# Half of one gate tile, a reordered square, moved sums and inner values, and two unread products in a decoder in fp32

## The reference, cut to what matters

```
x = x + 0.5 * swiglu_ffn(rmsnorm(x, ffn1_norm), w_gu, w_down)      # four FFNs in all, 2816 wide
x = x + mixer(rmsnorm(x, mix_norm))
# rglru, in the first mixer; w_r, w_i are 8 blocks of 64 x 64 each
r  = sigmoid(x @ w_r + b_r);  ig = sigmoid(x @ w_i + b_i)
a  = exp(-8 * r * softplus(-lam))
u  = sqrt(1 - a * a) * (ig * x);  h = scan(a, u)
# mlstm: h = (p @ v) / max(|sum p|, exp(-m)), p = exp(d - m) * (q @ k.T)
# second: mod = silu(c) @ ada_w + ada_b;  h = modulate(rmsnorm(ctx or x), mod) ...
```

## Time and profile before

| | us |
|---|---|
| median of 3 runs | 2051.26 (2048.83 to 2052.66) |
| the profiled execution | 2049.97 |
| its span, first to last instruction | 2048.2 |
| PE busy | 2018.8 |
| POOL busy | 1686.9 |
| DVE, ACT busy | 1156.3, 1147.0 |
| granted TensorE clock | 0.999 of full |

### The profile page before, as it was taken

The page is one execution under the profiler, slowest core; times in us unless marked ns, Lnnn a source line. Parts: engine busy times, 40 slices in busy tenths (PEclk is TensorE's granted clock), DMA queues, the critical chain, the costliest instruction groups (busy, mean ns, idle before and its releaser), DMA issues. The chain is left out here.

```text
span 2048.2 us, 38776 instructions
## 1 busy us (share of the span) xinstructions
PE 2018.8 (99%) x15616; PEld 1905.6 (93%) x15616; DVE 1156.3 (56%) x1985; ACT 1147.0 (56%) x1951; POOL 1686.9 (82%) x787
## 2 busy tenths in 40 slices
PE   9999999999999999999999999999999999999998
PEld 9999889999999977999889999999999998888886
DVE  7777635776577554444656315998788522222224
ACT  6445765435444466444754545457887655555555
POOL 4998778999899756889766586798777799999997
PEclk9999999999999999999999999999999999999999
DMA  9565446666766432666453355355454456555554
GB/s 356 211 223 185 151 169 229 232 210 231 270 249 223 183 127 102 252 218 222 167 196 128 144 184 217 105 186 186 165 166 165 166 186 201 194 192 194 195 193 146
DMA packets 80755, 395.28 MB, mean 193 GB/s; under 512 B 11100, under 2 KB 12252, under 8 KB 52448
## 3 DMA queue, kind: packets, MB, share of 16 engines
q1 hardware_dynamic: 80608, 393.28, 54.6%
HBM read 392.19 MB, written 1.05 MB: 192 GB/s over the span
## 5 line engine op out<-in xcount | busy, mean ns | idle before, releaser
L475 POOL TENSOR_TENSOR ring_low<-ring_raw,ring_high 128x2048 fp32r<-128x2048 f32 x204 | 998.5, 4913 | 230.3 <-ACT ring_high L461 230.2
L2668 POOL TENSOR_TENSOR peerS_low<-peerS_raw,peerS_high 128x512 fp32r<-128x512 f32 x510 | 655.6, 1310 | 88.0 <-ACT peerS_high L2819 87.7
L522 PE MATMUL bank<-keep_xThigh,ring_high 128*128 128x256 f32 x2080 | 581.6, 280 | 4.3 <-POOL ring_low L475 3.1
L523 PE MATMUL bank<-keep_xTlow,ring_high 128*128 128x256 f32 x2080 | 576.2, 277 | 0.0
L524 PE MATMUL bank<-keep_xThigh,ring_low 128*128 128x256 f32 x2080 | 576.2, 277 | 0.0
L461 ACT ACTIVATE ring_high<-ring_raw 128x2048 fp32r<-128x2048 f32 x204 | 391.1, 1917 | 271.9 <-PE bank L524 251.2
L522 PEld LDWEIGHTS bank<-keep_xThigh,ring_high 128*128 128x128 f32 x2080 | 391.0, 188 | 8.0 <-issue 5.1
L523 PEld LDWEIGHTS bank<-keep_xTlow,ring_high 128*128 128x128 f32 x2080 | 391.4, 188 | 0.3
L524 PEld LDWEIGHTS bank<-keep_xThigh,ring_low 128*128 128x128 f32 x2080 | 390.7, 188 | 0.0
L2819 ACT ACTIVATE peerS_high<-peerS_raw 128x512 fp32r<-128x512 f32 x510 | 320.5, 629 | 117.2 <-PE bank L524 96.7
L522 PE MATMUL bank<-keep_xThigh,peerS_high 128*128 128x256 f32 x1024 | 286.8, 280 | 0.9 <-POOL peerS_low L2668 0.8
(11 more groups left out here) (562 smaller groups left out, 3750.9 us busy)
## 6 DMA issues: line engine op xcount, KB each, us to landing
ring_raw<-in_stream SPq DMA_DIRECT2D x215, 1024.0 KB, 4.8
peerS_raw<-in_experts SPq DMA_DIRECT2D x256, 512.0 KB, 3.7
modcols_w<-in_ada_cols SPq DMA_DIRECT2D x32, 512.0 KB, 5.7
modlate_w<-in_ada_cols SPq DMA_DIRECT2D x8, 512.0 KB, 5.7
modcols_rows<-in_cond_rows SPq DMA_DIRECT2D x3, 1024.0 KB, 7.0
start_x<-in_x SPq DMA_DIRECT2D x2, 512.0 KB, 4.4
ring_raw<-in_stream SPq DMA_DIRECT2D x4, 256.0 KB, 6.2
context_in<-in_ctx SPq DMA_DIRECT2D x1, 1024.0 KB
```

The source lines that it names most:

```text
L475: self.nc.gpsimd.tensor_tensor(low_, self.raw_slot(n), high.bitcast(F32), ALU.subtract).then_inc(self.low_done.sem, 1)
L522: mm(out, sh, mh, start=start, stop=False)
L523: mm(out, sh, ml, start=False, stop=False)
L2668: g_.tensor_tensor(low[:, m % 2, cut], xraw[:, m % 3, cut], high[:, m % 2, cut].bitcast(F32), ALU.subtract).then_inc(made_low.sem, 1)
```

## The change

- `width`: of the tile AB_RG, ACT and POOL make halves of the first 1024 columns only.
- The columns of the first FFN are 0 to 6, from group 3 on; those of the second 7 to 15, from group 1 on.
- The 64 bytes between h0 and h1 in the first FFN go, and the inner values of group 0 move by 192 bytes, so that all inner values lie 192 bytes behind a multiple of 256.
- Behind the sum of the second to fourth FFN, `settle_pace`.
- In the mixer, a squared is made straight behind the four exponentials, into u's place, then the four tanh, then the tile's high half.
- The weighted values of heads 0 to 2 stand behind the first of the four row blocks of the output gate's first tile, those of head 3 behind the second.
- The sums of second stand in unit 1, ahead of its third row block.

```diff
@@ -47,7 +47,8 @@
 FILL = {"experts": (10, 11)}
-COLUMNS = {"1A": range(0, 8), "2A": range(8, 16), "1B": range(16, 32), "2B": range(32, 40)}
+COLUMNS = {"1A": range(0, 7), "2A": range(7, 16), "1B": range(16, 32), "2B": range(32, 40)}
+FIRST_GROUP = {"1A": 3, "2A": 1, "1B": 2, "2B": 2}
@@ -421,6 +422,11 @@
+    @staticmethod
+    def width(n):
+        return TILE // 2 if n == G_AB + AB_RG else TILE
@@ -458,7 +464,8 @@
             act.wait_ge(*self.released_at(self.before(n), loop * RAW))
-        self.nc.scalar.activation(self.parts(n)[0], self.raw_slot(n), ACT.Copy).then_inc(self.high_done.sem, 1)
+        cut = slice(0, self.width(n))
+        self.nc.scalar.activation(self.parts(n)[0][:, cut], self.raw_slot(n)[:, cut], ACT.Copy).then_inc(self.high_done.sem, 1)
@@ -472,7 +479,8 @@
             pool.wait_ge(self.high_done.sem, loop + self.highs(n))
-            self.nc.gpsimd.tensor_tensor(low_, self.raw_slot(n), high.bitcast(F32), ALU.subtract
+            cut = slice(0, self.width(n))
+            self.nc.gpsimd.tensor_tensor(low_[:, cut], self.raw_slot(n)[:, cut], high[:, cut].bitcast(F32), ALU.subtract
@@ -764,15 +772,15 @@
         for s in range(2):
-            work.at += 64 * (first and s)
...
-                   .rearrange("p (c t) -> p c t", c=2) for n, at in (("high", 0), ("low", 8 * T)))
+                   .rearrange("p (c t) -> p c t", c=2) for n, at in (("high", 192), ("low", 8 * T + 192)))
...
-        each = len(COLUMNS[part]) // (N - 3)
-        columns = lambda i: COLUMNS[part][each * (i - 2):each * (i - 1)]
+        i0 = FIRST_GROUP[part]
+        each = len(COLUMNS[part]) // (N - 1 - i0)
+        columns = lambda i: COLUMNS[part][each * (i - i0):each * (i - i0 + 1)] if i >= i0 else ()
@@ -793,8 +801,8 @@
                 early(sp)
-            for i in range(2, N - 1):
-                self.loads(sp, g0 + FFN_TILES, end=g0 + 3 * i + 4)
+            for i in range(1, N - 1):
+                self.loads(sp, g0 + FFN_TILES, end=max(g0 + 3 * i + 4, self.next_load))
@@ -861,6 +869,7 @@
                 self.sums_pe(pe, 4)
+                self.settle_pace(ps[2][:, 0:P])
@@ -978,6 +987,8 @@
                 self.prepare_vector(dve)
+            for n in columns(1):
+                mod.column(dve, n, part)
@@ -1200,7 +1211,7 @@
             g_ = nc.gpsimd
-            pool.wait_ge(*mod.summed.at(mod.sums(8)))
+            pool.wait_ge(*mod.summed.at(mod.sums(COLUMNS["1A"][-1] + 1)))
@@ -1220,13 +1231,15 @@
-            def rows_half(n, half):
+            def rows_half(n, half, between={}):
...
+                    if k in between:
+                        between[k]()
@@ -1311,17 +1324,24 @@
             rows_half(16, 1)
-            pe.wait_ge(*vmade.at(2))
-            for h in range(4):
-                pe.wait_ge(*pready.at(4))
-                if h == 3:
-                    pe.wait_ge(*hn.at(1))
+            def weighted_values(h):
...
-            rows_half(18, 0)
+            def first_values():
+                pe.wait_ge(*vmade.at(2))
+                pe.wait_ge(*pready.at(4))
+                for h in range(3):
+                    weighted_values(h)
+            def last_values():
+                pe.wait_ge(*hn.at(1))
+                weighted_values(3)
+            rows_half(18, 0, {1: first_values, 2: last_values})
@@ -1397,11 +1417,13 @@
             for c in range(4):
-                s_.activation(a[:, c, :], r[:, c, :], ACT.Exp, scale=negc[:, c:c + 1])
-                s_.activation(uP[c], r[:, c, :], ACT.Tanh, scale=posc[:, c:c + 1]).then_inc(decays.sem, 1)
+                s_.activation(a[:, c, :], r[:, c, :], ACT.Exp, scale=negc[:, c:c + 1]).then_inc(decays.sem, 1)
+            act.wait_ge(*decays.at(4))
+            s_.activation(u, a, ACT.Square)
+            for c in range(4):
+                last = s_.activation(uP[c], r[:, c, :], ACT.Tanh, scale=posc[:, c:c + 1])
+            last.then_inc(decays.sem, 1)
...
-            act.wait_ge(*decays.at(4))
-            s_.activation(r, a, ACT.Square).then_inc(decays.sem, 1)
@@ -1519,7 +1541,7 @@
             for b in range(2):
-                ins = v_.scalar_tensor_tensor(u[:, 2 * b:2 * b + 2, :], r[:, 2 * b:2 * b + 2, :], 1.0, tanh[b],
+                ins = v_.scalar_tensor_tensor(u[:, 2 * b:2 * b + 2, :], u[:, 2 * b:2 * b + 2, :], 1.0, tanh[b],
@@ -2137,8 +2159,15 @@
                     pe.wait_ge(*freed.at(2 * n - 2))
+                def sums():
+                    pe.wait_ge(*self.reduced.at(2))
+                    self.settle(nc.tensor.matmul(ps[5][:, 0:T], self.ones, self.red, start=True, stop=True))
+                    nc.tensor.matmul(ps[5][:, T:2 * T], self.ones, red2, start=True, stop=True).then_inc(self.summed.sem, 1)
...
-                                 done, n + 1 == NU or units[n + 1][0] != v, {0: c.low, FIRST_X: self.xlow}.get(n))
+                                 done, n + 1 == NU or units[n + 1][0] != v, {0: c.low, FIRST_X: self.xlow}.get(n),
+                                 {2: sums} if n == 1 else None)
@@ -2178,10 +2207,6 @@
                 unit(n)
-                if n == 0:
-                    pe.wait_ge(*self.reduced.at(2))
-                    nc.tensor.matmul(ps[5][:, 0:T], self.ones, self.red, start=True, stop=True)
-                    nc.tensor.matmul(ps[5][:, T:2 * T], self.ones, red2, start=True, stop=True).then_inc(self.summed.sem, 1)
...

```

## The result

The changed kernel takes 2059.82 us (median of 17 runs, 2052.16 to 2064.74), the kernel before in the same sessions 2050.3 (2048.8 to 2053.67): ratio 1.0038, 95% interval 1.0028 to 1.0047. The single times of the changed kernel also lie 12.6 us apart, those of before 4.9: seven of the 17 are at 2052.2 to 2056.9, ten at 2058.7 to 2064.7. The profiled execution, one of the ten, took 2061.84 us, 11.87 more than that of before, and the following is about that one.

What follows compares the result with a forecast made beforehand. It took PE's own stream and its 29 us idle as the bound. Mixer, sums and pads gave -9.6; with the open FFN terms -6.2 or -7.2, about 2043.5 from 2049.97, stated as 2044.5 us, range 2038 to 2050.

Steps and rivals of the forecast that it cites:

- The mixer: First mixer: shorter gate halves, earlier square and covered values give -6.05 us in all, bounds 3 and 6.5.
- Columns 14 and 15: Mixer: low half of these column units is in time, though POOL and PE meet within 0.3 us.
- First inner values at byte 192: FFNs: 48 products take 5.44 instead of 5.76 us.
- The second FFN: Ninth column makes low halves late: small stops of 0.5 to 0.9 us, or +4.9 if the long step follows.
- The case I had as likeliest: One of the first two FFNs keeps the long step: -6.2 or -7.2 us, 2044.5 us forecast, chance 0.46.
- the first FFN: Behind its stop, with h1 moved, the step stays long (+2.9 us) or short (-2.5), long likelier, 6 to 4.
- second's sums: Second: PE reaches the sums 2.7 us later, so the wait for context_red and 0.15 of refill go: -1.25 us.
- the term for the pads and the first inner values: Second to fourth FFN: short steps behind the sum and faster first inner values, 0.77 us each, -2.3 for three.
- the pads don't settle the step: Rival: three FFNs stay long to their end, 6 us each, +13.6 in all, 2063 us; chance 0.06.
- theory T: From the experiments: the sum's fp32 pair turns the step over, the fp16 pair turns it back; 256-byte blocks leave it short.
- The last rival: Neither place nor pads matter, the steps change with something else: -7.3 us, 2042.7 us; chance 0.07.

Runs made afterwards that it cites:

- e12: The kernel before with only the first mixer's three changes (gate weights at half width, square ahead of tanh, values among gate rows): 2043.24 us, ratio 0.9964.
- e1: The changed kernel with second's two sums back behind unit 0: 2051.06 us, ratio 1.0006 to the kernel before.
- e11: The changed kernel plus one small unread ACT operation between second's root and the next high half: 2053.44 us, ratio 1.0014 to the kernel before.
- e8: The changed kernel with columns as before and second's sums in unit 1 ahead of its second row block: 2048.54 us, ratio 1.0014 to the kernel before.
- e3: The kernel before with only second's two sums moved to unit 1, ahead of its third row block: 2051.75 us, ratio 1.0009.
- e7: The changed kernel with each FFN's first inner values at a multiple of 256 bytes again: 2052.09 us, ratio 1.0015 to the kernel before.
- e10: e6 with second's sums in unit 1 ahead of its second row block and a small ACT operation behind the root: 2040.35 us, ratio 0.9953.
- e6: e4 with the first FFN's h1 and all first inner values at a multiple of 256 bytes again, pads kept: 2043.46 us, ratio 0.9967.
- e9: e4 with only h1 of the first FFN at a multiple of 256 bytes again: 2041.97 us, ratio 0.9955 to the kernel before.
- e2: The changed kernel with the columns of the first two FFNs as before: 2047.74 us, ratio 0.9986 to the kernel before.
- e4: The changed kernel with second's sums back behind unit 0 and the columns as before: 2044.79 us, ratio 0.998 to the kernel before.
- e5: e4 without the fp16 products behind the sums of the second to fourth FFN: 2055.4 us, ratio 1.0021 to the kernel before.
- e13: The kernel before with only the columns of the first two FFNs changed: 2050.9 us, ratio 0.9998.

## Why the prediction was wrong

By its own sum the prediction had the profiled execution at 2042.8 (-7.2) or 2043.8 (-6.2); it took 2061.8. Of the 19.1 us above the first, second has 10.3 and the third FFN 7.1; these are the two steps that failed.

**Right, with their sizes.** The mixer: no wait for abo_xclow, one of 1.14 us for the tile behind it (forecast 1.1), u on time, the values covered: -6.5 against -6.05, and -7.3 alone (e12). Columns 14 and 15, which I called the tightest, held. First inner values at byte 192: 5.44 us (326.39 - 320.95). The second FFN: DVE's step 2 starts at 340.15, 7.4 earlier than before, with PE 9.5 ahead: 2.1 us late, where I had said some 3. A low half was late by 0.1, though one tile later than I had worked out, and once instead of five times: with the long step a tile takes PE 5.65 us, and POOL at 5.6 keeps up. The long step held from there on. The case I had as likeliest, one of the first two FFNs long, is the one that the profile shows (first short, second long). By its sum that would be -7.2. For the first FFN this was luck: I had long as likelier, 6 to 4.

**Wrong, first: second's sums, "The root chain starts 1.45 later; what is late next is the next unit's tile".** The forecast -1.25 was +9.0 in the profile; by medians 8.8 (e1) and 6.4 (e11) of the changed kernel's time hang on it. I checked whether a tile would be late but not what the chain would meet. I had used the exclusive hold of POOL and DVE for the columns, and not here. The four starts behind the root could have been worked out from the trace of before (root 0.47, high half 1.92, reciprocal 1.75 with their gaps), and they put POOL and DVE both 2.36 us behind the root's start. Before, ACT's high half had waited 0.28 us for PE behind the root, since PE itself had stood still for context_red. With that wait gone, the 0.39 us of distance went as well. The Trainium skill (SBUF — State Buffer, Who interferes with whom) has GpSimd and a VectorE operation with two SBUF inputs exclude each other, the first to be issued for its whole instruction. By that rule, the traces agree: 4.88 against 0.42 for the same squaring, and 4.92 against 4.60 for POOL in e8. About half of the 9.0 came on top: the clock at 0.50 and the wait for PTb, which e3 and e7 lack (163.5 and 163.4).

**Wrong, second: the term for the pads and the first inner values took the pads to settle the step, and "the pads don't settle the step" had 0.06.** I had seen fp16 products followed by short steps, and sums followed by long ones, and read two settings in it. But in the trace of before the sums of the later FFNs and of the second mixer had all found a short step, and the fp16 pairs a long one. One row of that trace spoke against it: the first FFN's sum, at 25.84, found the long step (117.8) and left the short one. The runs show a switch instead. In 31 of 31 places, over all profiles, where a sum stands in the last three FFNs or the second mixer without pads, the step behind it is the other one (eight times long to short), and so it is in the first FFN in all 16 (seven times long to short). In 33 of 33 places with sum and pads it is the same as ahead of it (29 short, four long).

That the fp16 pair is a second switch, as theory T has it, is not shown: with the sum it keeps the step, but alone it has no fixed effect. The middle one of the three places that had pads before, at 1314.22 in the trace of before, finds 117.8 (over the 18 steps ahead of it) in 15 of the 16 profiles; behind it the step is short in eight and long in seven. The 16th, e1, found it short and left it short. Behind it in the kernel before and in e10 (fp16 pair at 1303.69), after the same long step:

```profile
1316.00:1326.00 10.00, 10.00 (x91) 10.00 (x90) 9.79 (x17) 5.75 (x12) 9.93 (x9) 1.00 0.63 209
```

```profile
1305.00:1315.00 10.00, 10.00 (x87) 10.00 (x87) 9.76 (x19) 5.32 (x10) 9.59 (x8) 1.00 0.65 212
```

What sets it, whatever it was, is a block of inner values at a multiple of 256 (e6, e7, e9): behind all 52 such blocks without a stop inside, over all profiles, the step is short, and 20 of them had found it long. So the pads did for the three FFNs what was meant as long as all was short (-0.57 us in the second FFN of e2 and e4, 180.72 to 180.15; I had said 0.77, without the 0.19 that the sum is longer with pads behind it), and moving the first inner values took away the only thing that would have ended a long step: +6.3 in the third FFN. The rival had named this price, 6 us each, but for a pad that fails, not for one that keeps what it finds. The last rival, by which neither place nor pads matter, falls: e5, e7 and e9 move the spacing or the spread with one of them at a time, at a granted clock of 1.00. Its other half, that the step changes with something else, is true beside them: stops of 0.1 us or less can turn it.

**Open.** The 1.2 us in the second mixer are a drop of the clock: 0.51 from 722.70 to 726.10, behind 32 narrow products of 32 columns, worth 1.6 us (144.95 in e1 against 143.34 in e11, with the same steps). Six of 16 profiles have it (after, e1, e2, e3, e9, e12), the kernel before's not; no run here looked for its cause. A drop of the same length stands behind the first FFN's stop in e2 and e9 and in the first mixer in e3 and e13. Which way the step falls behind a stop is open as well: with h1 moved, the first FFN was short in six of eight profiles behind a stop of 1.1 to 2.2 us at the same place. What the fp16 pair alone does is open too. And what physically makes the two spacings wasn't tried.

## What to carry to other kernels

Two events that used to be ordered by a wait are not ordered any more when the wait is removed. Work out the next few starts on every engine to the hundredth, above all for engines that exclude each other, and put a deliberate distance where they fall together. A state that lasts (here a spacing) must be read with what it was before each event, not only after it; "followed by" is no rule until both starts have been seen. Time the parts of a bundle alone: here one part was worth -7.3 us, two others together +15 (e4).

## What was not expected of the hardware

The step between 256-column products has two values, 113.3 and 117.8 ns, at one granted clock. The sum, a pair of fp32 products with ones in the trace, turns it over (47 of 47 places). The same sum with two fp16 products behind it leaves it as it was (33 of 33), though the fp16 pair alone has no fixed effect. A block of 48 products whose moving values lie at a multiple of 256 bytes takes 5.74 to 5.76 instead of 5.44 us and leaves the step short (52 of 52). A PE stop of 0.1 us or less can turn it.

DVE's squaring of the root took 0.42 us in the one profile where it started 3 ns behind POOL's low half, and 4.88 in the four where it started 5 to 10 ns behind. Stops of PE of 3.6 us came with the clock at 0.50 for 6.8 us, from within the stop, in two profiles; stops of 3.4 us at the same place came without it in two others.
